# The experts' dispatch and return as two rounded products each, in place of one fp32 product

## The reference

```python
def moe(x2, w_router, router_bias, w1, w3, w2):
    expert_idx, gate_w = route(x2, w_router, router_bias)   # 2 of 16 experts for each token
    ...
    def run_block(args):
        e, toks = args
        xb = x_pad[toks]                                    # dispatch: tokens to slots
        h = jax.nn.silu(xb @ w1[e]) * (xb @ w3[e])
        return h @ w2[e]
    ...
    y = yb.reshape(-1, D) * slot_gate[:, None]
    return jnp.zeros((N + 1, D), x2.dtype).at[slot_tok].add(y)[:N]   # return: slots to tokens
```

## Time and profile before

| | |
|---|---|
| median of 3 runs | 2011.35 us (2008.25 to 2012.51) |
| the profiled execution's own time | 2013.33 us |
| its span, first to last instruction | 2011.8 us |
| PE busy | 1753.5 us, 87% of the span |
| DVE, ACT busy | 774.0 us (38%), 642.6 us (32%) |
| read from memory | 390.07 MB |

### The profile page before, as it was taken

The page is one execution under the profiler, slowest core; times in us unless marked ns, Lnnn a source line. Parts: engine busy times, 40 slices in busy tenths (PEclk is TensorE's granted clock), DMA queues, the critical chain, the costliest instruction groups (busy, mean ns, idle before and its releaser), DMA issues.

```text
span 2011.8 us, 22089 instructions
## 1 busy us (share of the span) xinstructions
PE 1753.5 (87%) x9214; PEld 1288.5 (64%) x9214; DVE 774.0 (38%) x1476; ACT 642.6 (32%) x1041; POOL 29.5 (1%) x49
## 2 busy tenths in 40 slices
PE   6998986899997998986899995857899988588999
PEld 5777985444435777985444434844599977447997
DVE  4445343210115545333210015643455545515554
ACT  3326422010004336422011013443344444415442
POOL 4000000000000000000000000000000000000000
PEclk9998998799998998998899997965899998678999
DMA  8332345499995432335499992510255545003552
GB/s 258 138 126 93 147 147 219 176 401 421 421 420 178 153 125 89 147 147 218 173 414 421 421 421 99 197 40 0 84 189 188 178 142 183 1 21 126 189 189 105
DMA packets 57663, 392.67 MB, mean 195 GB/s; under 512 B 7124, under 2 KB 7168, under 8 KB 15696
## 3 DMA queue, kind: packets, MB, share of 16 engines
q1 hardware_dynamic: 54144, 380.30, 49.4%
q0 software_dynamic: 3264, 9.61, 1.4%
q10 hardware_dynamic: 144, 1.24, 0.2%
HBM read 390.07 MB, written 1.05 MB: 194 GB/s over the span
## 4 chain that ended last, share of the span: by engine, by line
PE 79%; DVE 10%; ACT 5%; DMA 4%; issue 2%; SPq 0%; DVEq 0%; ACTq 0%
PE psum L538 76%; DMA ring_sb<-in_weights 4%; PE psum L664 2%; ACT ring_rounded L1127 1%; DVE ring_rounded L1469 1%; PE psum L583 1%; ACT region_sb L1153 1%; DVE x_sb L1580 0%; ACT xT_hi_rounded L1352 0%; DVE x_sb L1578 0%; DVE region_sb L1853 0%; DVE region_sb L1856 0%; DVE small_sb L1849 0%; ACT region_sb L1341 0%; DVE region_sb L1847 0%
## 5 line engine op out<-in xcount | busy, mean ns | idle before, releaser
L538 PE MATMUL psum<-ring_sb,region_sb 128*64 128x512 f32 (+1 forms) x1728 | 427.0, 599 | 14.9 <-ACT region_sb L1341 11.0
L1469 DVE TENSOR_TENSOR ring_rounded<-ring_sb,ring_rounded 128x2048 fp32r<-128x2048 f32 (+4 forms) x152 | 321.5, 2130 | 245.6 <-ACT ring_rounded L1127 245.4
L538 PE MATMUL psum<-xT_hi_rounded,ring_rounded 128*128 128x256 f32 x1920 | 357.9, 288 | 0.0
L1127 ACT ACTIVATE ring_rounded<-ring_sb 128x2048 fp32r<-128x2048 f32 (+4 forms) x152 | 268.1, 1781 | 212.7 <-PE psum L538 149.9
L538 PEld LDWEIGHTS psum<-ring_sb,region_sb 128*64 128x64 f32 (+1 forms) x1728 | 148.2, 144 | 277.5 <-issue 260.1
L538 PE MATMUL psum<-ring_rounded,xT_hi_rounded 128*128 128x384 f32 (+4 forms) x960 | 278.3, 367 | 37.1 <-DVE ring_rounded L1469 18.1
L538 PE MATMUL psum<-xT_lo_rounded,ring_rounded 128*128 128x256 f32 x960 | 285.8, 298 | 27.9 <-DVE ring_rounded L1469 16.8
L538 PEld LDWEIGHTS psum<-xT_hi_rounded,ring_rounded 128*128 128x128 f32 x1920 | 308.3, 197 | 1.8 <-issue 0.5
L538 PEld LDWEIGHTS psum<-ring_rounded,xT_hi_rounded 128*128 128x128 f32 x960 | 184.4, 198 | 61.9 <-issue 39.4
L538 PEld LDWEIGHTS psum<-xT_lo_rounded,ring_rounded 128*128 128x128 f32 x960 | 189.7, 198 | 31.6 <-issue 18.1
L538 PE MATMUL psum<-ring_rounded,region_rounded 128*128 128x512 f32 x768 | 178.7, 392 | 3.0 <-DVE region_rounded L2055 3.0
(11 more groups left out here) (239 smaller groups left out, 1345.1 us busy)
## 6 DMA issues: line engine op xcount, KB each, us to landing
ring_sb<-in_weights SPq DMA_DIRECT2D x324, 1024.0 KB, 7.8
ring_sb<-in_weights SPq DMA_DIRECT2D x24, 768.0 KB, 4.3
ring_sb<-in_weights SPq DMA_DIRECT2D x8, 904.0 KB, 4.5
ring_sb<-in_weights SPq DMA_DIRECT2D x8, 900.0 KB, 4.6
ring_sb<-in_weights SPq DMA_DIRECT2D x8, 584.0 KB, 14.3
region_sb<-in_mem POOLq DMA_DIRECT2D x2, 1024.0 KB, 8.5
region_sb<-in_pool_band POOLq DMA_DIRECT2D x2, 1024.0 KB, 10.0
region_sb<-in_ln_g POOLq DMA_DIRECT2D x4, 512.0 KB, 4.3
```

The source lines that it names most:

```text
L538: return nc.tensor.matmul(dst, lhsT, rhs, start=first, stop=last, skip_group_check=True)
L1127: nc.scalar.activation(rounded(piece.hi), piece.raw, ACT.Copy).then_inc(hi_made, 1)
L1469: nc.vector.tensor_tensor(rounded(piece.raw), piece.raw, reread(piece.hi), ALU.subtract).then_inc(lo_made, 1)
```

## The change

The one-hot matrix holds 0 and 1, so one rounded operand holds it whole. The other operand of each product is split in two: an upper part, rounded to fp32r, and the rounded rest. So each unsplit fp32 product of the dispatch and of the return becomes two fp32r products.

- Dispatch: ACT copies x to `x_upper` (behind `act_xT`), DVE subtracts it from x to `x_lower` (behind `vec_xT`), once a layer. PE waits for both before the first dispatch.
- Return: `expert_out` was written by DVE alone. Now ACT writes the upper part (bank times gate, rounded), signals, and only then DVE writes the rest (bank times gate minus the upper part). The bank is free after DVE's.
- `sel` and `selT` are written as fp32r; other readers of `sel` read the same bytes as fp32, and their products are as before.
- Several semaphores of the second block are now those of the first block, counted on (`signal_after`); they were renamed. This adds no wait.

```diff
         def pe_dispatch(l, quarter):
...
                 pe.wait_ge(*sel_made.last(l))
+                pe.wait_ge(*x_upper_made.last(l))
+                pe.wait_ge(*x_lower_made.last(l))
                 pe.wait_ge(*free)
                 for j in range(2):
                     for b in range(TB):
-                        last = matmul(psum[:, i, j * S:(j + 1) * S], x[:, b, (c + j) * P:(c + j + 1) * P],
-                                      flat_sel[:, b, quarter * S:(quarter + 1) * S], b == 0, b == TB - 1)
+                        chosen = rounded(flat_sel[:, b, quarter * S:(quarter + 1) * S])
+                        matmul(psum[:, i, j * S:(j + 1) * S], rounded(x_lower[:, b, (c + j) * P:(c + j + 1) * P]), chosen, b == 0, False)
+                        last = matmul(psum[:, i, j * S:(j + 1) * S], rounded(x_upper[:, b, (c + j) * P:(c + j + 1) * P]), chosen, False,
+                                      b == TB - 1)
...
         def pe_gather(l, pair):
-            sT, y = selT[pair % 2], expert_out[pair % 2]
+            sT, y, y_rest = selT[pair % 2], expert_out[pair % 2], y_lower_rows[pair % 2]
...
-                    last = matmul(held[:, b, half * BANK:(half + 1) * BANK], sT[:, b, :], y[:, half * BANK:(half + 1) * BANK],
-                                  pair == 0, pair == PAIRS - 1)
+                    cols = slice(half * BANK, (half + 1) * BANK)
+                    matmul(held[:, b, cols], rounded(sT[:, b, :]), rounded(y_rest[:, cols]), pair == 0, False)
+                    last = matmul(held[:, b, cols], rounded(sT[:, b, :]), rounded(y[:, cols]), False, pair == PAIRS - 1)
...
         def scalar_experts(l):
             E = N_EXPERTS
             act_xT(l, 1)
+            for b in range(TB):
+                a.wait_ge(*x_normed.at(l, b))
+                nc.scalar.activation(rounded(x_upper[:, b, :]), x[:, b, :], ACT.Copy).then_inc(x_upper_made.sem, 1)
...
+                    y = expert_out[(pair - 1) % 2]
+                    for half in range(2):
+                        i, full = loose.of(("y", l, pair - 1, half))
+                        a.wait_ge(*full)
+                        a.wait_ge(*slot_gated.last(l))
+                        nc.scalar.activation(rounded(y[:, half * BANK:(half + 1) * BANK]), psum[:, i, :], ACT.Copy,
+                                             scale=slot_gate[:, pair - 1:pair]).then_inc(y_upper_made.sem, 1)
...
             vec_xT(l, 1)
+            for b in range(TB):
+                v.wait_ge(*x_upper_made.at(l, b))
+                nc.vector.tensor_tensor(rounded(x_lower[:, b, :]), x[:, b, :], reread(x_upper[:, b, :]), ALU.subtract).then_inc(x_lower_made.sem, 1)
...
-                        v.wait_ge(*full)
-                        nc.vector.tensor_scalar(y[:, half * BANK:(half + 1) * BANK], psum[:, i, :], slot_gate[:, pair - 1:pair], None,
-                                                ALU.mult).then_inc(gated.sem, 1)
+                        cols = slice(half * BANK, (half + 1) * BANK)
+                        v.wait_ge(*y_upper_made.at(l, (pair - 1) * 2 + half))
+                        nc.vector.scalar_tensor_tensor(rounded(y_rest[:, cols]), psum[:, i, :], slot_gate[:, pair - 1:pair], reread(y[:, cols]),
+                                                       ALU.mult, ALU.subtract).then_inc(gated.sem, 1)
```

More of the change, by code:

```diff
@@ L463, in signal, with signal_after @@
             return Signal(sem(name), per_layer)
+        def signal_after(first, per_layer):
+            return Signal(first.sem, per_layer, first_layers * first.per_layer)
         x_in, consts_in, params_in, router_in, positions_in, out_stored = (
@@ L894, in pe_experts_down @@
             for b in range(TB):
[L895 removed]
+                last = nc.tensor.transpose(psum[:, i, b * P:(b + 1) * P], reread(flat_sel[:, b, pair * P:(pair + 1) * P]), ident)
             last.then_inc(full, 1)
@@ L1337, in scalar_experts @@
                     a.wait_ge(*full)
-                    nc.scalar.activation(selT[(pair - 1) % 2].rearrange("p b t -> p (b t)"), psum[:, i, 0:S], ACT.Copy).then_inc(spread.sem, 1)
+                    nc.scalar.activation(rounded(selT[(pair - 1) % 2].rearrange("p b t -> p (b t)")), psum[:, i, 0:S], ACT.Copy).then_inc(spread.sem, 1)
                     i, full = loose.of(("rowsT", l, pair - 1))
```

42 lines of the change are left out of this document (23 added, 19 removed).

## The result

| | before | changed | ratio, 95% interval |
|---|---|---|---|
| median, first measurement (4 runs each) | 2009.80 us | 1995.57 us | 0.993 [0.9913, 0.9947] |
| median, repeated later beside other kernels (12 and 5 runs) | 2010.89 us | 1995.52 us | 0.9917 [0.9903, 0.9931] |
| span of the profiled execution | 2011.8 us | 1995.5 us | |
| PE busy | 1753.5 us | 1706.3 us | |

A forecast was written before the change was run, and what follows sets the result against it. PE and the weight loads at 421 GB/s were taken as level in the experts' stages. Terms of 7.2 + 3.0 + 0.85 made 11.0 us, so 2011.35 - 11.0 = 2000.4 us, range 1994.5 to 2008.

The forecast's parts named there:

- The frame: Experts' stage can't be shorter than its first release, plus 210 us of loading, plus PE's work behind pair 6's last landing.
- the three signs: Forecast wrong if the 210 us moves, stage clock is below 0.95, or DVE's idle before its first sum changes kind.
- Term 1, the start: First dispatch ahead of each layer's first load shortens, 3.6 us a layer, 7.2 us in both (5.8 to 8.8).
- Term 2, the holes: Gaps in the weight stream behind a dispatch and return, 2.6 and 0.9 us, go: 3.0 us taken (1.3 to 3.5).
- Term 3, behind the landing: Pair 6's return gives 1.0 us a layer, DVE's later final sum takes some back: 0.85 us together (-1 to 2).
- PE's saved work: Over 8 dispatches and 16 returns PE loses 55 us of work, nearly all hidden inside the 210 us of loading.
- the rival in which PE alone is the bound: Loads had room, so all 55 us come back: 1956 us; 2%.
- The clock did not fall in the gaps where PE waits for loads: Rival: in the stages PE's clock falls in these gaps, at half of the time costing 28 us: 2028 us; 4%.
- The jump kept its length in both layers: Rival: DVE's branch after the last pair changes cost; layer 0's dear, 4.5 us more, 2008 with low terms; 10%.
- Rounded products were as fast with these operands: Rival: dispatch and return products don't get faster or run as two records, 55 us added, near 2060; 2%.
- a cheap jump in layer 1: Rival: DVE's branch over the late tokens after layer 1's last pair becomes cheap: 1995.9 us; 6%.

The follow-up runs named there:

- Experiment 1: Changed kernel with the return as one fp32 product as before, only the dispatch as two rounded products: 2001.22 us against 2012.48 for the kernel before.
- experiment 3: Kernel before with only each layer's first dispatch as two rounded products, other dispatches and the return fp32: 2005.61 us against 2012.48.
- experiments 4 and 5: Changed kernel, then kernel before, each with half of the experts' weight loads left out and PE's work the same: 1966.03 and 2006.57 us against 2010.89.
- kernel 6: Changed kernel with 54 extra products a layer keeping PE busy ahead of the first dispatch: 1994.73 us against 2012.48 for the kernel before.
- the delays: Changed kernel with 1.25 us, then 3.4 us, of added DVE work in the norm behind layer 1's experts: 2002.12 and 2000.68 us against 2009.97.
- all but the split: Changed kernel with PE kept busy, 80 DVE copies and pair 6's late return, first dispatch not split: 1985.72 us against 2012.50 for the kernel before.
- kernels 1 to 3: Experiment 1; changed kernel with the dispatch as one fp32 product, only the return rounded (2006.42 us against 2012.48); experiment 3.
- kernel 7: Changed kernel with 80 one-element copies added on DVE in layer 1's stage, ten to a pair: 1995.39 us, ratio 0.9923 to the kernel before.
- experiment 10: Changed kernel with all steps: PE kept busy, 80 DVE copies, first dispatch split, pair 6's return late: 1991.60 us against 2009.97 for the kernel before.

## Why the prediction was right, and where it was not

**The frame** held to 0.2 us: 210.19 and 210.00 us from first issue to pair 6's last landing in the changed kernel, 210.0 forecast. Experiment 1 (the whole gain of the stages without the return's part of PE's savings), experiment 3 (6.8 of the 41 us of savings, two thirds of the gain) and experiments 4 and 5 (loads halved: 32 us come out of the changed kernel, 1.6 out of the one before) show that the loads are what bounds it now. None of the three signs by which the forecast would have been wrong came: the 210 us stayed, the clock from first issue to landing is 0.99 in both layers, and DVE's idle time is of the same kind as before.

**Term 1, the start:** 3.34 + 3.42 = 6.8 us, forecast 7.2. The first dispatch took 6.39 us and not 6.1:

```profile
367.60 6.39 PE L547 MATMUL psum<-region_rounded 128*128 128x256 f32 x32 [2.97 <-DVE region_rounded L1818]
```

```profile
367.60:373.99 6.39, 6.39 (x32) 6.19 (x32) 0.00 (x0) 1.79 (x3) 0.00 (x0) 0.59 0.00 0
```

The new parts of x were covered, as said: the first dispatch starts 4.42 us behind the six small products, 4.43 before, and ACT's copies took 1.05, DVE's subtractions 1.22 us.

**Term 2, the holes:** 2.36 + 0.98 = 3.3 us, forecast 3.0.

**Term 3, behind the landing:** 0.11 and -0.05 us, forecast 0.85. This is the term that was mis-sized. Pair 6's return gave 8.76 - 7.91 = 0.85 us and not 1.0 between the landing and pair 7's w2. At the end I had let DVE's sum into x start only 0.35 to 0.4 us later in layer 0, as if the 0.41 us of idle time ahead of it were a wait for PE that the rest's longer way would cover. Behind the change 0.43 us of idle time stand there with no releaser, so the jump by itself takes as long; before, its end and PE's fell together. From ACT's start at 603.64 to the sum at 605.54 it is 1.90 us, from the gate's start to the sum it was 1.17, so 0.73 us are lost. In layer 1 it is the same 0.73, and the jump took 5.11 us in place of 4.91.

**The sum** of the stages is 10.2 us against 11.0. Term 1 fell short by 0.4 us and term 3 by 0.8, and term 2 gave 0.3 more.

**PE's saved work** was over-sized: 55 us forecast, 40.6 measured (experiments 4 and 5), and PE's waits for the loads 24.4 us, not 40. The page's PE busy fell by 47.2 us. I multiplied 16 returns by 1.75 us, though the prediction itself says that a return without a dispatch ahead of it, 10 of the 16, waits for DVE. It cost nothing in the forecast, since that work is hidden; the rival in which PE alone is the bound would have come out 14 us too fast.

**The rivals.** The clock did not fall in the gaps where PE waits for loads: 1.00 in the window of 460 to 520 us, with PE busy for 89% and no gap for a load over 1.33 us. The Trainium skill (TensorE: Matmul & The Clock Gate, "HAM oscillation — how this bites in real kernels") describes waits longer than the bursts between them; none of these rows has that case, and they don't speak against the section. The jump kept its length in both layers. Rounded products were as fast with these operands as in the earlier trace rows.

**The rest of the span** gave 6.3 us between the profiled executions, which no step of the prediction has. So the hit is in part luck: with the bounds of its three terms alone the prediction has 1997 to 2005.5 us, and 1995.57 lies below that. The range holds it only because it was widened down to 1994.5 for a cheap jump in layer 1, which did not come. Of the 6.3 us, 781.37 - 775.43 = 5.9 lie behind layer 1's experts, on unchanged code. Windows at the same work, first of the kernel before, then of the changed one (the first 16 us behind the turn of x, and 10 us from 114.5 us behind it):

```profile
1230.47:1246.47 16.00, 9.41 (x35) 9.04 (x36) 10.36 (x13) 11.21 (x17) 0.00 (x0) 0.51 0.00 0
1345.00:1355.00 10.00, 9.42 (x50) 7.45 (x49) 3.87 (x19) 2.88 (x6) 0.00 (x0) 0.67 0.00 0
```

```profile
1220.02:1236.02 16.00, 9.17 (x42) 8.96 (x43) 10.29 (x13) 11.13 (x18) 0.00 (x0) 0.70 0.00 0
1334.55:1344.55 10.00, 10.00 (x79) 8.12 (x78) 4.53 (x19) 4.65 (x10) 0.00 (x0) 0.96 0.01 2
```

The granted clock is higher at both places (79 products against 50 in 10 us). The same windows over the whole stretch, before and changed:

```profile
1230.47:2011.70 781.23, 667.56 (x3632) 564.78 (x3632) 377.94 (x668) 326.72 (x522) 0.00 (x0) 0.87 0.34 120
```

```profile
1220.02:1995.40 775.38, 661.31 (x3632) 559.50 (x3632) 377.97 (x668) 326.85 (x522) 0.00 (x0) 0.88 0.34 121
```

The same 3632 products keep PE busy for 6.3 us less, while DVE's and ACT's busy times are the same. Behind layer 1 the profiled executions took 775.4 us (changed, twice), 775.7 (kernel 6), 775.8 and 776.4 (the delays), 776.7 (all but the split), against 781.4 (before), 782.9, 782.8 and 781.1 (kernels 1 to 3), 781.4 (all steps) and 780.3 (kernel 7); the two with half loads lie between (779.5 changed, 778.7 before). So the difference is the clock's. What decides it is open: it follows neither the amount by which PE is early nor the code behind it, kernel 7 took 780.3 us with a clock of 0.65 in its first 16 us, and the delays didn't settle it. The medians point to a part that belongs to the kernel and not to one execution, but don't show it: kernel 1 has the same stages as the changed one and a median 5.7 us higher, measured beside a kernel before that was 1.6 us higher too, and the intervals of the ratios overlap (0.9937 [0.9919, 0.9955] and 0.9917 [0.9903, 0.9931]).

## What to carry to other kernels

Where PE and the stream of weights are level, work taken from PE pays only where the stream stands: ahead of its first release, in holes, and behind its last landing. Find these places and cost them alone; here they gave 10 us of 41. Keeping PE busy through a short wait ahead of them (5.0 us), putting work behind the last landing into the wait for it (2.6 us) and moving a jump to where it is cheap (4.9 us) gave 12 us more in the stages, while an earlier first release bought with a later second one gave holes instead. And a change of 0.7% in a program whose clock steps up and down must be read from the milestones of the profile, since unchanged code elsewhere moved by 6 us.

## What the runs showed of the hardware

**A jump's cost depends on where it starts.** Counted in the program, DVE jumps on by 216 instructions, ACT by 132. The same jump left its engine idle for 0.04 to 0.44 us or for 4.9 to 5.3 us, over all kernels here. The page's third part shows how instructions are fetched:

```profile
q8 instruction: 76, 1.25, 0.2%
...
q14 instruction: 35, 0.29, 0.0%
```

0.29 MB in 35 packets are 8 KB each. Taken as 128 instructions (an estimate), and with 65 instructions ahead of the program (fitted to the first two profiles), a jump is long where (start + 65) modulo 128, plus the jump, reaches 256:

| jump, starts in the program at | remainder + jump | idle behind it |
|---|---|---|
| DVE 476 and 478 (layer 0, before and after) | 245, 247 | 0.41, 0.43 us |
| DVE 1146 and 1150 (layer 1, before and after) | 275, 279 | 4.91, 5.11 us |
| DVE 1230 (layer 1, kernel 7) | 231 | 0.16 us |
| ACT 316 (layer 0, before), 318 (layer 0, kernels 1 and 3) | 257, 259 | 5.00, 5.03, 5.05 us |
| ACT 335 (layer 0, after), 757 (layer 1, before) | 148, 186 | 0.26, 0.16 us |

Kernel 7 was made by this rule and came out as it says; that the place decides is shown, the rule fits all rows, and why it holds is argued. The trace has packets of this queue some 3 us behind short and long jumps alike (three at 1202.9 to 1203.1 us in kernel 7, whose jump starts at 1200.4; three at 1204.6 to 1204.9 in the changed kernel, whose jump starts at 1201.9), so it doesn't show by itself that only the long one waits for a fetch. The Trainium skill (Runtime: NRT & Kernel Launch, "Instruction fetch mechanics") has the mechanism, a taken branch whose target isn't in the two blocks held waits for a fetch. Its blocks are 16 KiB, 256 instructions; with the one in use and the next of that size held, no jump of 132 or 216 could miss. The packets of 8 KB and the lengths of these jumps agree with half that size, which is what the table goes by.

**A first dispatch behind idle time runs at half speed for much of its length** (6.39 us at granted clock 0.59, against 4.04 us at 1.00 with PE kept busy, the same 32 products). Products whose results nobody reads, run while PE would stand, win this back: the first dispatch is 2.4 us shorter and the first load comes 3.0 us sooner, in each layer.

**A PE that the profile shows as busy can lose its clock.** Behind the 32 products of only 16 columns for the slots' gates, the granted clock falls to 0.50 for some us in layer 0 of every kernel, without a wait for loads or another engine: 0.63 over 392.4 to 397 us in the changed kernel, with PE busy throughout. Where the fall lasted longer, a hole in the stream of weights stood behind it (experiment 10).
